# Two-layer hybrid decoder step on one core: transposes, their copy and the output products of block attention moved to later rounds, with a third buffer of probabilities

## The reference, cut to what matters

```python
logits = jnp.einsum('bhqd,bhqnkd->bhqnk', q_c, kg) * scale
mask = val_c[..., None] & (kpos <= pos_c[None, None, :, None, None])
logits = jnp.where(mask, logits, NEG)
w = jax.nn.softmax(logits.reshape(bsz, nh, qc, nsel * MOBA_BLOCK), axis=-1).reshape(logits.shape)
return jnp.einsum('bhqnk,bhqnkd->bhqd', w, vg)
```

## Time and profile before

| | us |
|---|---|
| median of 3 runs | 1878.08 |
| lowest, highest | 1874.36, 1878.15 |
| the profiled execution | 1887.05 |
| its span, first to last instruction | 1885.3 |
| PE busy (share of the span) | 1787.7 (95%) |
| DVE busy | 1134.8 (60%) |
| ACT busy | 734.1 (39%) |
| mean granted TensorE clock | 0.966 |

### The profile page before, as it was taken

One profiled execution on the slowest core, in us unless ns is written; L12 is line 12 of the kernel. 1 busy time (PEld: TensorE's weight loads), 2 busy tenths in 40 slices (PEclk: granted clock), 3 DMA queues, 4 the chain that ended last, 5 costly groups with the idle time before them and its releaser, 6 DMA issues.

```text
span 1885.3 us, 34376 instructions
## 1 busy us (share of the span) xinstructions
PE 1787.7 (95%) x13464; PEld 1622.6 (86%) x13464; DVE 1134.8 (60%) x2371; ACT 734.1 (39%) x1321; POOL 36.0 (2%) x65
## 2 busy tenths in 40 slices
PE   6899798999999999999999998888999999999997
PEld 5789455999999999989799985445999999999997
DVE  7975356568777762256525855666468777762264
ACT  5222335553333342256323323656553333342253
POOL 1400000000000000000000000000000000000000
PEclk9999788999999999999999996989999999999999
DMA  4124577313222232132121142863313222132111
GB/s 182 66 28 163 204 267 288 112 43 100 79 88 78 64 132 81 47 118 79 51 95 57 57 150 96 313 225 122 111 35 98 81 79 88 54 136 79 71 64 51
DMA packets 77953, 204.18 MB, mean 108 GB/s; under 512 B 12530, under 2 KB 14882, under 8 KB 77314
## 3 DMA queue, kind: packets, MB, share of 16 engines
q1 hardware_dynamic: 75762, 190.36, 29.8%
q0 software_dynamic: 2064, 12.06, 1.7%
HBM read 190.81 MB, written 10.40 MB: 107 GB/s over the span
## 4 chain that ended last, share of the span: by engine, by line
PE 86%; DVE 8%; ACT 2%; issue 2%; DMA 2%; SPq 1%; DVEq 0%; ACTq 0%; POOLq 0%
PE psum L412 29%; PE psum L1946 15%; PE psum L606 13%; PE psum L2346 7%; PE psum L2303 3%; PE psum L420 3%; PE psum L1408 2%; PE psum L1383 2%; PE psum L865 2%; PE psum L2496 1%; PE psum L526 1%; PE psum L540 1%; PE psum L1492 1%; PE psum L1520 1%; PE psum L2559 1%
## 5 line engine op out<-in xcount | busy, mean ns | idle before, releaser
L412 PE MATMUL psum<-sb_a_sb_r,sb_ring_r 128*128 128x288 f32 x1408 | 297.6, 296 | 0.0
L412 PE MATMUL psum<-sb_a_sb_r,sb_arena_r 128*128 128x288 f32 x1344 | 276.5, 296 | 0.0
L412 PE MATMUL psum<-sb_y_sb_r,sb_ring_r 128*128 128x288 f32 x960 | 263.3, 299 | 0.6 <-DVE sb_ring_r L372 0.6
L412 PEld LDWEIGHTS psum<-sb_a_sb_r,sb_ring_r 128*128 128x128 f32 x1408 | 231.3, 188 | 0.3
L372 DVE TENSOR_TENSOR sb_ring_r<-sb_ring,sb_ring_r 128x1024 fp32r<-128x1024 f32 (+1 forms) x90 | 116.2, 1295 | 177.7 <-ACT sb_ring_r L369 176.7
L412 PEld LDWEIGHTS psum<-sb_a_sb_r,sb_arena_r 128*128 128x128 f32 x1344 | 217.0, 188 | 0.0
L412 PE MATMUL psum<-sb_y_sb_r,sb_arena_r 128*128 128x288 f32 x704 | 207.2, 294 | 6.3 <-DVE sb_a_sb_r L372 6.2
L369 ACT ACTIVATE sb_ring_r<-sb_ring 128x1024 fp32r<-128x1024 f32 (+1 forms) x90 | 99.9, 1114 | 289.2 <-PE psum L412 172.3
L412 PEld LDWEIGHTS psum<-sb_y_sb_r,sb_ring_r 128*128 128x128 f32 x960 | 175.5, 190 | 1.5 <-DVE sb_ring_r L372 1.0
L369 ACT ACTIVATE sb_arena_r<-sb_ring 128x1024 fp32r<-128x1024 f32 x90 | 92.9, 1055 | 171.6 <-PE psum L412 149.5
L606 PE MATMUL psum<-sb_arena_r 128*128 128x288 f32 x960 | 156.9, 297 | 1.0 <-DVE sb_arena_r L372 0.9
(11 more groups left out here) (406 smaller groups left out, 3176.3 us busy)
## 6 DMA issues: line engine op xcount, KB each, us to landing
sb_ring<-w SPq DMA_DIRECT2D x166, 512.0 KB, 3.5
sb_ring<-wd SPq DMA_DIRECT2D x32, 704.0 KB, 4.2
sb_arena<-sb_v SPq DMA_DIRECT2D x64, 256.0 KB, 5.3
sb_arena<-moba_v SPq DMA_DIRECT2D x56, 256.0 KB, 5.3
sb_ring<-moba_k SPq DMA_DIRECT2D x32, 256.0 KB, 5.6
sb_a_sb<-moba_k SPq DMA_DIRECT2D x32, 256.0 KB, 7.5
sb_ring<-sb_k SPq DMA_DIRECT2D x32, 256.0 KB, 6.0
sb_a_sb<-sb_k SPq DMA_DIRECT2D x32, 256.0 KB, 6.5
```

Of the source, the lines that this page charges most:

```text
L412: ins = e.eng.matmul(out[:, half, :], fr(w[p][:, k, :]), fr(x[q][:, k, cols]), start=(first and k == 0 and i == 0), stop=(last and k == kb ...
```

## The change

PE issues the transposes of unit u-2 instead of u-1 in round u, and the output products of units u-5 and u-4 instead of u-3 and u-2. ACT copies the transposes of unit u-3 instead of u-1. `pb` gets a third buffer, so the exponential of unit u waits for the transposes of unit u-3 instead of u-2. The copy out per pair of heads moves from round 10 + 8 c to 12 + 8 c. PE now has two more rounds after the last unit (36 instead of 34) and ACT two more (35 instead of 33). The samples' pieces stay in the rounds in which they were, except those that the last round picked up.

```diff
-        pb = [cut(unit_at + i * 512, 512) for i in range(2)]
+        pb = [cut(unit_at + i * 512, 512) for i in (0, 1, 6)]
+        assert unit_at + 7 * 512 <= 27952
...
-            for u in range(len(UNITS) + 2):
+            for u in range(len(UNITS) + 4):
                 if u + 1 < len(UNITS):
                     scores(u + 1)
-                if 1 <= u <= len(UNITS):
-                    hh, i = UNITS[u - 1]
-                    pe.wait_ge(pn_ready, u)
-                    if u >= 3:
-                        pe.wait_ge(pt_ready, u - 2)
-                    for j in range(i + 1):
-                        last = pe.transpose(psum[:, 2 + (u - 1) % 2, j * P:(j + 1) * P],
-                                            pb[(u - 1) % 2][:, j * P:(j + 1) * P], ident)
+                if 2 <= u < len(UNITS) + 2:
+                    k = u - 2
+                    pe.wait_ge(pn_ready, k + 1)
+                    if k >= 2:
+                        pe.wait_ge(pt_ready, k - 1)
+                    for j in range(UNITS[k][1] + 1):
+                        last = pe.transpose(psum[:, 2 + k % 2, j * P:(j + 1) * P], pb[k % 3][:, j * P:(j + 1) * P], ident)
                     last.then_inc(ptr_ready, 1)
-                if u >= 3 and u % 2 == 1:
-                    outputs(u - 3)
-                between(samples, u, len(UNITS) + 1, DUE_A["pe"])
+                if u >= 5 and u % 2 == 1:
+                    outputs(u - 5)
+                between(samples, u, len(UNITS) + 3, DUE_A["pe"])
...
-            for u in range(len(UNITS) + 1):
+            for u in range(len(UNITS) + 3):
...
-                    if u >= 2:
-                        act.wait_ge(ptr_ready, u - 1)
-                    act.activation(pb[u % 2][:, 0:n], psum[:, u % 2, 0:n], ACT.Exp, scale=ATT_SCALE,
+                    if u >= 3:
+                        act.wait_ge(ptr_ready, u - 2)
+                    act.activation(pb[u % 3][:, 0:n], psum[:, u % 2, 0:n], ACT.Exp, scale=ATT_SCALE,
...
-                if u >= 1:
-                    hh, i = UNITS[u - 1]
-                    act.wait_ge(ptr_ready, u)
-                    if u >= 5:
-                        act.wait_ge(o_unit, u - 4)
-                    act.activation(ptb[(u - 1) % 4][:, 0:i + 1, :], psum[:, 2 + (u - 1) % 2, 0:P * (i + 1)]
+                if u >= 3:
+                    k = u - 3
+                    i = UNITS[k][1]
+                    act.wait_ge(ptr_ready, k + 1)
+                    if k >= 4:
+                        act.wait_ge(o_unit, k - 3)
+                    act.activation(ptb[k % 4][:, 0:i + 1, :], psum[:, 2 + k % 2, 0:P * (i + 1)]
                                    .rearrange("p (j n) -> p j n", j=i + 1), ACT.Copy).then_inc(pt_ready, 1)
-                if u >= 10 and (u - 10) % 8 == 0:
-                    copy_out((u - 10) // 8)
-                if u == len(UNITS):
+                if u >= 12 and (u - 12) % 8 == 0:
+                    copy_out((u - 12) // 8)
+                if u == len(UNITS) + 2:
                     act_slab(e, out_pairs[1], 1)
                     copy_out(3)
-                between(samples, u, len(UNITS), DUE_A["act"])
+                between(samples, u, len(UNITS) + 2, DUE_A["act"])
```

More of the change, by code:

```diff
@@ L1585, in dve_moba_prompt @@
                     do(v.reciprocal(stat[:, 6 + w % 2:7 + w % 2], stat[:, 4 + w % 2:5 + w % 2]))
-                    v.tensor_scalar(pb[w % 2][:, 0:n], pb[w % 2][:, 0:n], stat[:, 6 + w % 2:7 + w % 2], None, ALU.mult)\
+                    v.tensor_scalar(pb[w % 3][:, 0:n], pb[w % 3][:, 0:n], stat[:, 6 + w % 2:7 + w % 2], None, ALU.mult)\
                      .then_inc(pn_ready, 1)
```

## The result

The changed kernel is slower. Median 1886.83 us in 13 runs (1878.22 to 1894.51) beside 1878.07 us of the kernel before in 13 (1872.50 to 1886.52); ratio 1.0048, 95% interval [1.0029, 1.0066], so +5.4 to +12.4 us. A second set of 10 runs gave 1.0047 [1.0028, 1.0065]. Forecast were no change, 1877.8 us, and 1872.5 to 1883.

A forecast was written before the change was run, and what follows sets the result against it. Each period was taken as bound by a DVE-then-ACT chain up to the softmax, then by PE alone. Terms -2.6 - 0.4 - 0.6 + 2.3 + 1.0 = -0.3 us on the 1878.1 us median gave 1877.8; range 1872.5 to 1883.

The forecast's parts named there:

- The wait is replaced, not removed: Key products to softmax: PE waits for exponentials and the softmax instead of the division; DVE and ACT part doesn't shorten.
- The lag: Sample-weight transposes (L1397) start 0.79 to 0.98 us behind the softmax; some 0.25 stays of each, gain 2.6 us.
- First rounds: Unit 0's transpose moves from before the first key products to behind them: gain 0.4 us.
- The end: After the last sample-weight transposes PE has more moved work, +1.07 us; copies covered, -0.1; total +1.0 us.
- The clock: Full clock returns 3.7 us after each L1397 starts instead of 2.55: 0.57 us lost a period, +2.3 us in all.
- the sum: All terms against the profiled execution: -2.6 - 0.4 - 0.6 + 2.3 + 1.0 = -0.3 us.
- Rival 1: Clock returns late, 6.96 us after each L1397 starts: +6.2 us, 1884.3 us; chance 0.14.
- Rival 2: PE stays at full clock in the attention stage, fewer waits in a row: -7.7 us, 1870.4 us; chance 0.10.
- The range: Whole run: 1872.5 to 1883 us, leaving out some 0.1 on each side.

The follow-up runs named there:

- e10: Changed kernel plus throwaway PE products in every gap: 4 and 8 per period, 5 more for pair 0; ratio 0.9973 to the kernel before, stage 111.4 us.
- e11: Kernel before plus 4 and 9 throwaway PE products in rounds 4 and 5 of every period; ratio 0.9965 to the kernel before, stage 109.9 us.
- e1: Changed kernel plus 9 and 18 throwaway PE products per period, overfilling its gaps; ratio 1.0082 to the kernel before, stage 131.2 us.

## Why the prediction was wrong

- *The wait is replaced, not removed*: right. In the third period, for which it was worked out, PE waits 1.10 and 2.09 us at the places and within 0.2 us of the lengths forecast (0.9 and 2.1). DVE and ACT need the same 10.0 us. The lag gave 3.3 us (10.92, 10.93, 10.74 and 10.81 us from key products to L1397 became 10.0 each), forecast 2.6.
- *First rounds*: 0.1 us instead of 0.4.
- *The end*: from the last L1397 to the next stage 10.96 became 12.24 us. Of these 1.28, 0.5 is clock; the rest, 0.8, was forecast as 1.0. `act_out_first` held nothing.
- *The clock*: this step failed, by size, and with it the sign of the whole. It said "I take 3.7, the row that is most like it" for the return behind L1397. It came after 7.7, 6.1, 8.6 and 3.2 us, mean 6.4: (6.4 - 2.55) / 2 x 4 = 7.7 us instead of 2.3. With that the sum is -0.3 + 5.4 = +5.1, beside +4.1 in the stage's profile and +8.8 in the runs; from L1397 to the next key products the three full periods took 16.91, 16.67 and 16.65 us before and 18.99, 18.17 and 19.36 after, +6.3. Rival 1, with 6.96 us and 1884.3, was the one that came true by its mechanism, at a chance of 0.14; its +6.2 us, too, is short of the runs' +8.8.
- Why 3.7 was the wrong row: I counted the return from the start of dense work. At 217.35 the clock had already been at half since 210.8, so that row holds only the end of a stretch of 10.2 us. And the fall had moved. It used to come 4.4 to 7.7 us before L1397 (mean 6.0), so that more of each half-clock stretch lay over waits; now it comes 1.7 to 5.9 us before it (mean 3.9), in the wait right before L1397 in the third period and in or just after the wait for an exponential in the others. The stretches also became longer, 10.3 us in the mean instead of 8.5. Of the 3.9 us by which the return came later, the fall's place makes 2.1 and the length 1.8. No run shows why they became longer. For the first of these the rows were there: the earlier trace rows give both ends of each stretch, and I used only the later one.
- *Rival 2* was taken for a wish: its full clock would have needed the gaps filled, and with them filled it is worth two thirds of what it said (-7.7 forecast, -5.1 in e10). By the Trainium skill ("TensorE: Matmul & The Clock Gate", What's actually happening), activity releases the throttle. e10 and e11 agree in so far as the clock, once full, stayed full over such work; e1 doesn't, where PE was busy without a gap for 23.8 us and the clock stayed at half.
- *The range* was made around one execution and one stage. With the return as measured the forecast would have been 1878.1 + 5.1 = 1883.2 us, still 3.6 below the median of 1886.8; no term of the sum allowed for more half clock outside the stage.

## What to carry to other kernels

Before work is taken out of a gap on PE, ask where the idle time goes: half clock over a wait costs nothing, half clock over dense work costs about half of the time it covers, and the place of the gap shifts the one to the other. Read both ends of every half-clock stretch against the dense work, and where a chain of DVE and ACT sets a gap's end anyway, try filling the gap: 13 throwaway products per period, in two rounds of the old order, won 6.6 us, the whole reordering lost 8.8. Fit the fill to the gap; too little won nothing, too much gave the gain back. And fill while the clock is still full: in e1's first period the fill ran at half clock, took nearly twice as long and did not end it.

## What was not expected

- 72 value products with 32-column weights took 2.24 us at full clock and 4.06 us when all but the last 0.2 us of them stood at half clock (1.8 times), so their time follows the granted clock nearly in full; I had left this open.
- A product of the identity with 64 columns in fp32 shows as two instructions of 0.11 us, as long as a transpose of 128 columns costs for each further block (0.11).
- Identical code in the recurrence of layer 1 took 42.1 to 52.7 us in eighteen profiles. One profile against one profile can't show a change of 9 us in this kernel.
